# A two-layer decoder trunk on one core: the gate table's one-hot products in fp32r, built four tokens at a time between u tiles

## The reference

```python
D_MODEL, SEQ, DEPTH = 1024, 256, 2
PEER_HEADS, N_KEYS, PEER_TOPK = 8, 128, 16          # 128 x 128 = 16384 experts

def peer_ffn(h, w_query, sub_keys1, sub_keys2, expert_u, expert_v):
    ...
        q = (xb @ w_query).reshape(PEER_BLOCK, PEER_HEADS, 2, PEER_HALF)
        s1 = jnp.einsum('thd,kd->thk', q[:, :, 0], sub_keys1)
        s2 = jnp.einsum('thd,kd->thk', q[:, :, 1], sub_keys2)
        v1, i1 = lax.top_k(s1, PEER_TOPK)
        v2, i2 = lax.top_k(s2, PEER_TOPK)
        cand = (v1[..., :, None] + v2[..., None, :]).reshape(PEER_BLOCK, PEER_HEADS, PEER_TOPK * PEER_TOPK)
        top, ci = lax.top_k(cand, PEER_TOPK)
        idx = (key of half 1) * N_KEYS + (key of half 2)
        gate = jax.nn.softmax(top, axis=-1)
        act = jax.nn.gelu(jnp.einsum('td,tkd->tk', xb, expert_u[idx]))
        return jnp.einsum('tk,tkd->td', gate * act, expert_v[idx])
```

## Time and profile before

| | us |
|---|---|
| median of 3 runs | 2143.91 (2143.36 to 2144.42) |
| the profiled execution, its own time | 2144.6 |
| its span, first to last instruction | 2142.8 |
| TensorE busy | 2086.6, 97% |
| VectorE busy | 1520.0, 71% |
| ScalarE busy | 976.5, 46% |
| GpSimd busy | 778.6, 36% |
| granted TensorE clock, mean | 0.993 |

### The profile page before, as it was taken

One profiled execution on the slowest core, in us unless ns is written; L12 is line 12 of the kernel. 1 busy time (PEld: TensorE's weight loads), 2 busy tenths in 40 slices (PEclk: granted clock), 3 DMA queues, 4 the chain that ended last, 5 costly groups with the idle time before them and its releaser, 6 DMA issues.

```text
span 2142.8 us, 45777 instructions
## 1 busy us (share of the span) xinstructions
PE 2086.6 (97%) x14382; PEld 1943.4 (91%) x14382; DVE 1520.0 (71%) x3212; ACT 976.5 (46%) x1363; POOL 778.6 (36%) x323
## 2 busy tenths in 40 slices
PE   7999999999999999999989999999999999999997
PEld 6999899999998888899889999999999988888996
DVE  3753159789878888777648431797989788886776
ACT  4644454554543333344355444545554433333443
POOL 5698669500000000244367986793000000003442
PEclk9999999999999999999999999999999999999999
DMA  7355457655557777655453554576555687776553
GB/s 234 123 184 183 157 169 227 217 163 161 162 193 245 239 241 242 205 189 185 166 170 127 187 187 149 179 230 203 162 163 160 210 243 241 241 242 194 183 189 120
DMA packets 154706, 410.71 MB, mean 192 GB/s; under 512 B 16987, under 2 KB 67340, under 8 KB 154588
## 3 DMA queue, kind: packets, MB, share of 16 engines
q1 hardware_dynamic: 154220, 407.75, 59.9%
q0 software_dynamic: 368, 1.57, 0.2%
HBM read 382.00 MB, written 27.26 MB: 191 GB/s over the span
## 4 chain that ended last, share of the span: by engine, by line
PE 95%; ACT 1%; DVE 1%; issue 1%; DMA 0%; DVEq 0%; ACTq 0%
PE bank L1048 55%; PE bank L1245 32%; PE bank L1297 5%; PE bank L1223 1%; PE bank L1070 1%; PE bank L1146 0%; PE bank L1103 0%; PE bank L1207 0%; DVE area L748 0%; DVE hT L755 0%; DVE act L976 0%; PE bank L1144 0%; DVE coef L980 0%; DMA x<-in_x 0%; ACT area L485 0%
## 5 line engine op out<-in xcount | busy, mean ns | idle before, releaser
L444 POOL TENSOR_TENSOR halves<-ring,halves 128x1024 fp32r<-128x1024 f32 x308 | 772.4, 2520 | 1327.3 <-ACT halves L509 1325.5
L1048 PE MATMUL bank<-hT,halves 128*128 128x256 f32 x8688 | 1120.6, 285 | 10.8 <-DVE hT L755 9.0
L509 ACT ACTIVATE halves<-ring 128x1024 fp32r<-128x1024 f32 x668 | 707.3, 1060 | 888.0 <-PE bank L1048 468.7
L1048 PEld LDWEIGHTS bank<-hT,halves 128*128 128x128 f32 x8688 | 1068.3, 191 | 18.8 <-issue 9.8
L1245 PE MATMUL bank<-halves,coef 128*128 128x512 f32 x3072 | 711.7, 391 | 3.8 <-DVE coef L982 3.8
L1245 PEld LDWEIGHTS bank<-halves,coef 128*128 128x128 f32 x3072 | 573.3, 188 | 122.6 <-DVE coef L982 5.9
L943 DVE TENSOR_TENSOR halves<-ring,halves 128x1024 fp32r<-128x1024 f32 x360 | 438.9, 1220 | 61.0 <-ACT x L649 25.7
L976 DVE TENSOR_TENSOR act<-act,area 128x256 f32<-128x256 f32 x256 | 223.8, 874 | 99.6 <-ACT act L619 93.9
L956 DVE TENSOR_SCALAR onehot<-ids,x 128x128 f32<-128x128 f32 x512 | 173.7, 339 | 1.9 <-issue 1.9
L1297 PE MATMUL bank<-onehot,x 128*128 128x128 f32 x1024 | 156.0, 274 | 0.0
L955 DVE TENSOR_SCALAR x<-ids,x 128x128 f32<-128x128 f32 x512 | 143.1, 279 | 16.9 <-PE bank L1297 15.9
(11 more groups left out here) (137 smaller groups left out, 951.9 us busy)
## 6 DMA issues: line engine op xcount, KB each, us to landing
ring<-in_stream SPq DMA_DIRECT2D x672, 512.0 KB, 3.5
held_blocks<-act SPq DMA_DIRECT2D x188, 128.0 KB, 1.9
act<-held_blocks SPq DMA_DIRECT2D x188, 128.0 KB, 3.1
area<-rel_scratch SPq DMA_DIRECT2D x2, 1024.0 KB, 6.4
rel_scratch<-act POOLq DMA_DIRECT2D x1, 1532.0 KB, 14.5
area<-in_consts SPq DMA_DIRECT2D x2, 576.0 KB, 3.8
x<-in_x SPq DMA_DIRECT2D x1, 1024.0 KB, 5.0
out_y<-x SPq DMA_DIRECT2D x2, 512.0 KB, 2.7
```

The costliest lines, as they stand in the source:

```text
L444: pool.tensor_tensor(halves[:, s, 1, :], ring[:, s, :], halves[:, s, 0, :].bitcast(F32), ALU.subtract)\
L509: a.activation(halves[:, s, 0, :], ring[:, s, :], ACT.Copy).then_inc(hi_done, 1)
L1048: i = pe.matmul(o, stationary[a], moving[b], start=begin and n == 0, stop=end and n == len(TERMS) - 1)
```

## The change

Five things change together.

1. **The products.** `onehot2` gets a high and a low side: each token's moving operand is 256 columns wide, the gate's fp32r high part in 128 and the low part in the other 128, and the matmul runs in fp32r. The two sides of the result stand beside each other in the bank and are added on the way to `gates_t`: ScalarE copies the high side (`side`), VectorE adds the low side (`add_side`), for two tokens at a time.
2. **The one-hots.** They are made for four tokens at a time (a set, 64 for each layer) by VectorE with `tensor_tensor` on broadcast operands: mask (L992), low side (L996), `onehot1` (L997), weights on the mask's first two tokens (L999). ScalarE puts the weights on the other two (`weighted`). Keys and weights lie in PSUM banks 0 and 1.
3. **The stage.** It holds 64 u tiles in place of 48, one for each set, and GpSimd makes their lows. The main stage has 16 blocks in place of 32. The products' results go to four banks in place of two.
4. **x.** It goes to DRAM behind the mixing (issued on ScalarE's queue), comes back in the main stage, and is added at the end; the identity matmuls go.
5. **Layers.** They are written out in place of the loop.

```diff
-HELD = 48
+HELD = 64
...
+                a.dma_start(x_home, x[:, :, :]).then_inc(x_saved, 16)
...
-                        a.wait_ge(outer_done, l * NQ + j * BODY + (STEPS + 2 * (g4 + 1)))
-                        a.activation(gates_t[:, :, bass.ds(j * (2 * BODY) + 4 * g4, 4)],
-                                     bank_g[g4 % 2][:, :].rearrange("p (t e) -> p e t", t=4), ACT.Copy)\
-                            .then_inc(table_ready, 1)
...
+                def weighted(n):
+                    a.wait_ge(low_placed, l * SETS + n + 1)
+                    for u in range(2, FOUR):
+                        rows = onehot2[:, n % 2, u, 0, :]
+                        i = a.activation(rows, rows.bitcast(F32), ACT.Copy, scale=weight[:, n, u - 2:u - 1])
+                    i.then_inc(onehots_ready, 1)
...
+                def side(q):
+                    a.wait_ge(outer_done, l * NQ + q + 1)
+                    a.activation(gates_t[:, :, 2 * q:2 * q + 2],
+                                 bank_g[q % 4][:, :].rearrange("p (t h e) -> p h e t", t=2, h=2)[:, 0], ACT.Copy)\
+                        .then_inc(side_copied, 1)
...
+                weighted(0)
+                for n in range(SETS):
+                    if n >= 1:
+                        side(2 * n - 2)
+                        side(2 * n - 1)
+                    if n + 1 < SETS:
+                        weighted(n + 1)
+                    hold(n)
...
-                            v.tensor_scalar(onehot1[:, s, u, :], iota, key1, None, ALU.is_equal)
-                            i = v.tensor_scalar(onehot2[:, s, u, :], iota, key2, weight, ALU.is_equal, ALU.mult)
...
+                def add_side(q):
+                    v.wait_ge(side_copied, l * NQ + q + 1)
+                    g2 = gates_t[:, :, 2 * q:2 * q + 2]
+                    v.tensor_tensor(g2, g2, bank_g[q % 4][:, :].rearrange("p (t h e) -> p h e t", t=2, h=2)[:, 1], ALU.add)\
+                        .then_inc(table_ready, 1)
+                def onehots(n, between=None):
+                    if n >= 2:
+                        v.wait_ge(outer_done, l * NQ + 2 * (n - 1))
...
+                    v.tensor_tensor(hi, keys2, numbers, ALU.is_equal).then_inc(mask_ready, 1)
+                    if between is not None:
+                        add_side(between)
+                    v.wait_ge(mask_ready, l * SETS + n + 1)
+                    v.tensor_tensor(lo, hi.bitcast(F32), low_weights, ALU.mult).then_inc(low_ready, 1)
+                    v.tensor_tensor(onehot1[:, n % 2], keys1, numbers, ALU.is_equal)
+                    v.wait_ge(low_ready, l * SETS + n + 1)
+                    v.tensor_tensor(hi[:, 0:2], hi[:, 0:2].bitcast(F32),
+                                    weightT[:, n * FOUR:n * FOUR + 2].unsqueeze(2).to_broadcast([P, 2, NK]), ALU.mult)\
+                        .then_inc(low_placed, 1)
+                onehots(0)
+                onehots(1)
+                for n in range(1, SETS):
+                    if n + 1 < SETS:
+                        onehots(n + 1, 2 * n - 2)
...
+                    add_side(2 * n - 1)
...
+                for n in range(SETS):
+                    held(n)
+                    pe.wait_ge(onehots_ready, l * SETS + n + 1)
+                    for q in (2 * n, 2 * n + 1):
+                        if q >= 4:
+                            pe.wait_ge(table_ready, l * NQ + q - 3)
```

More of the change, by code:

```diff
@@ L341, in _ @@
                 sp.sem_inc(held_stored[k], 16)
-            with sp.Fori(0, DEPTH) as l:
+            for l in range(DEPTH):
                 sp.wait_ge(lo_pool, l * LOP + 1)
@@ L450, in low @@
                 subtract(s)
-            with pool.Fori(0, DEPTH) as l:
+            for l in range(DEPTH):
                 pool.wait_ge(params_ready, l + 1)
@@ L498, in roots @@
                 i.then_inc(root_ready, 1)
-            a.sem_inc(table_ready, 2)
             a.wait_ge(chain, 1)
-            with a.Fori(0, DEPTH) as l:
+            for l in range(DEPTH):
                 g = [0]
@@ L646, in _ @@
                     if s == SEL_AT:
[L647 to L650, removed]
+                        a.wait_ge(sel_turned, l + 1)
+                        a.wait_ge(x_saved, l * 16 + 16)
+                        a.activation(weight_hi, weightT, ACT.Copy).then_inc(weights_hi, 1)
@@ L674, in _ @@
+                side(NQ - 2)
+                side(NQ - 1)
                 for i in range(TAIL):
-                    hold(HELD, i)
+                    hold(HELD + i)
                 with a.Fori(0, EARLY // RING) as r:
@@ L716, in _ @@
             v.tensor_copy(relv, bank[0][:, 0:NDIST]).then_inc(rel_vector, 1)
-            with v.Fori(0, DEPTH) as l:
+            for l in range(DEPTH):
                 links = [1]
@@ L940, in low @@
+                onehots(0)
[3 more added lines that the diff above has]
+                        onehots(n + 1, 2 * n - 2)
+                    else:
+                        add_side(2 * n - 2)
+                    add_side(2 * n - 1)
+                add_side(NQ - 2)
+                add_side(NQ - 1)
                 def low(n, s):
@@ L1022, in _ @@
             pe.wait_ge(rel_vector, 1)
-            with pe.Fori(0, DEPTH) as l:
+            for l in range(DEPTH):
                 g = [0]
@@ L1204, in _ @@
                 pe.wait_ge(taken_v, l * NGV + taken_before(first("h2T"))[0])
-                for t in range(TT):
-                    for hf in range(2):
-                        pe.matmul(acc[2 * t + hf][:, :], ident, x[:, t, hf * HALF_N:(hf + 1) * HALF_N], start=True,
-                                  stop=True)
                 pe.wait_ge(diag_ready, l * 2 + 2)
@@ L1295, in _ @@
+                for n in range(SETS):
[4 more added lines that the diff above has]
+                            pe.wait_ge(table_ready, l * NQ + q - 3)
                         for u in range(2):
-                            o = (2 * q + u) % 4 * NK
-                            i = pe.matmul(bank_g[g4 % 2][:, o:o + NK], onehot1[:, s, u, :], onehot2[:, s, u, :],
-                                          start=True, stop=True)
+                            row = 2 * (q % 2) + u
+                            i = pe.matmul(bank_g[q % 4][:, u * S:(u + 1) * S], onehot1[:, n % 2, row, :],
+                                          onehot2[:, n % 2, row].rearrange("p h k -> p (h k)"), start=True, stop=True)
@@ L1299, in _ @@
                         i.then_inc(outer_done, 1)
-                        for c in range(CHUNKS * q, CHUNKS * (q + 1)):
-                            held(j * PER, c // KD, [c % KD])
                 for i in range(TAIL):
-                    held(HELD, i, range(KD))
-                with pe.Fori(0, EARLY // RING) as r:
+                    held(HELD + i)
+                for s in range(RING):
+                    v_product(s, s, s % 2, opens=s == 0)
+                with pe.Fori(1, EARLY // RING) as r:
```

147 lines of the change are left out of this document (73 added, 74 removed).

## The result

| | us |
|---|---|
| median before, 4 runs | 2144.06 (2143.36 to 2144.42) |
| median after, 4 runs | 2207.52 (2202.33 to 2208.82) |
| ratio, 95% interval | 1.029 (1.0277 to 1.0303) |
| the profiled execution of the kernel after, its own time | 2208.1, span 2206.1 |

The page of the kernel after, parts 1 and 4: busy time by engine, and the chain that ended last.

A forecast was written before the change was run, and what follows sets the result against it. TensorE bound the kernel (busy 97%, 95% of the chain); the change would make a ScalarE-VectorE circle the table stage's pace. 2144.6 - 54 (products) + 108 (waits) + 3 (clock) = 2201 us, range 2160 to 2250.

The forecast's parts named there:

- The products, 54.3 us of gain: Table stage, one-hot products: a pair falls from 0.45 to 0.238 us on TensorE, 256 pairs, 54.3 us less work.
- The work of the others below that: Table stage, one set: VectorE 2.85, ScalarE 2.36, GpSimd 2.4 us of work, all below TensorE's 3.33.
- The circle, 4.25 us: Table stage: ScalarE and VectorE wait for each other, one set each 4.25 us (4.0 to 4.6); chance 0.80.
- A lead of 5 us, a loss of 108: Table stage: TensorE waits 0.92 us for each of 64 sets, less a 5 us lead; 54 us a layer, 108.
- 3 us for the clock at the transposes: Transposes, identity matmuls gone: TensorE idles some 4 us and the clock falls; 1.5 us a layer, 3 in all.
- x through DRAM, written-out layers, 0: Saving and reloading x lies beside other work, bound 0 to 5 us for each layer; written-out layers nothing.
- Vector operations unstretched: Table stage: VectorE's operations with one PSUM operand aren't lengthened by GpSimd's lows; the rival, 2300 to 2430 us, chance 0.05.
- The clock in the stage: Table stage: clock stays 1.00; a rival had it fall at TensorE's stops, 2500 us if throughout, chance 0.03.
- The signs of being wrong: Table stage: no TensorE gaps, 512-column VectorE operations much over 0.69 us, or copies costing more than a 256-column GELU.
- Where TensorE's gap would show: Table stage: TensorE idle 0.9 us in each set ahead of the one-hot products, released by ScalarE's weighting.
- The rival that ended faster: Table stage: copies needn't wait behind high and GELU, circle 3.03 us, TensorE stays the bound; 2094 us, chance 0.09.
- The clock rival: Table stage: TensorE's short stops drop the clock to the 1.2 GHz level; 2500 us throughout, 2300 for a third; chance 0.03.

The follow-up runs named there:

- the second experiment: Against the changed kernel, ScalarE does a tile's high and GELU ahead of the weightings instead of behind them: 2097.45 us.
- the first experiment: Against the changed kernel, VectorE's first adding of a low side is moved from behind the mask to behind the weights: 2092.74 us.
- the dense version: Against the changed kernel, high-side copies and low-side addings work on 256 floats side by side instead of pairs 1 KB apart: 2194.35 us.
- the three versions that break the circle: Against the changed kernel: first adding behind the weights, 2092.74 us; high and GELU ahead of the weightings, 2097.45; VectorE weighting all four tokens, 2097.57.

## Why the prediction was right, step by step

- **TensorE's work was the bound.** Right: with the circle cut, it is again.
- **The products, 54.3 us of gain.** Mis-sized by 3 us. The new pair took 0.24 us, as forecast. But a u matmul takes 0.120 us (2.88/24), not 0.119, so nine of them leave 0.44 of the old step of 1.52 us for the old pair, and 256 x 0.20 = 51 us. The stage says the same: with the circle cut (the second experiment) its pieces take 232.3 us, and 232.3 - 45.9 is 25.5 less than 211.9, in each of two layers. The whole time of the first experiment lies 2145.61 - 2092.74 = 52.9 us below the kernel before (on the same chip), with everything else that changed in it.
- **3.33 us for a set on TensorE.** 3.36 us.
- **The work of the others below that.** Right, and no bound, as the prediction went on to say.
- **The circle, 4.25 us.** 4.30 us, with the same members in the same order. The adding of a side was mis-sized: 0.42 from start to start (504.14 to 504.56) against 0.34, by the order of its accesses; the dense version has 0.34. Small terms the other way (0.59 for the two weightings against 0.62, 1.19 for two operations of 512 columns against 1.22) make up for part of it. High (0.95), low side and `onehot1` (0.59 and 0.60) and the GELU's step (0.27) were the rows' values.
- **A lead of 5 us, a loss of 108.** TensorE's stage was 288.0 us in each layer; with the high first (the second experiment) the same pieces of the chain, 416.04 to 648.34, were 232.3. The loss is 55.7 in each layer, 111 in all, and 64 x 0.94 - 55.7 leaves a lead of 4.5 us. In the timeline TensorE first waits at 435.28, behind the fifth group of products, where the prediction's walk put it. The relay runs from 420.89 to 688.53, 267.6 us against a forecast of some 267. (The 48 tiles of the stage before are a quarter fewer than 64, not a third.)
- **3 us for the clock at the transposes.** In the kernel after, the 32 transposes took 6.78 us in one layer; in the other, 16 of them 3.37, where it was 1.80 before. Between the same two pieces of the chain around them (97.66 to 412.25, before 100.09 to 412.64) a layer is 2.0 us longer, and in the second layer 1.2 (1195.70 to 1509.48, before 1161.20 to 1473.75). Right.
- **x through DRAM, written-out layers, 0.** Right for x. From the first v product to the last product of the main stage, 398.9 us in the first layer (700.28 to 1099.14). That is 128 v tiles at 2.72 and 16 u tiles at 2.87, 394 us, and the gap where the main stage begins, which the kernel before had too. No row waits for x. Elsewhere the profiled execution was 5 us shorter than that of the kernel before: 2.4 ahead of the long piece of the first layer (97.66, before 100.09), and 2.7 behind the first v product of the second (408.7 us to the end of the span, before 457.2, of which 45.9 have moved). No run says which change or which clock they come from.
- **Vector operations unstretched.** Right: 686 to 692 ns for 512 columns all through the stage.
- **The clock in the stage.** It stayed at 1.00 with 0.94 us of stops in each 4.30, so the swing that the Trainium skill ("TensorE: Matmul & The Clock Gate", section on psum-queue depth-cycling) describes did not show in the changed kernel.
- **The signs of being wrong.** One of them showed: the copies cost more than a GELU of 256 columns (439 ns on average against 363). It hardly touched the circle. The first copy lets VectorE start 0.41 us after its own start (503.73 to 504.14), against 0.40 forecast; the second is the long one, 0.49 us (499.70 in the timeline), and lies beside the path.
- **Where TensorE's gap would show.** Wrong in the place: I had it ahead of the one-hot products, released by the weightings. It stands ahead of the u tile (503.97), released by the GELU two tiles back; ahead of the products (506.96) only 0.1 us is left. Both are members of the circle, so the size was untouched.

Between 2201 and 2207.5 lie 6.5 us, and more than one term was off. The stage's loss was 111 in place of 108 and its gain 51 in place of 54, 6 us together. The token mixing of the second layer took 4.8 us more (1105.44 to 1195.70, before 1075.73 to 1161.20), which the forecast did not have, and the 5 us less at other places nearly cancel that: this part of the agreement is luck. Most of the 4.8 us is, in the profiled execution, a clock that fell once more. The attention's logit matmuls of the second layer took, in the chain of the kernel after:

```profile
41.34 4.07 PE bank L1157 x30
...
1134.51 7.53 PE bank L1157 x30
```

and 4.07 in both layers before. (The granted clock was 0.59 and 0.50 from 1134 to 1142, and 1.00 at the same matmuls before.) Over the other profiled kernels the same 30 matmuls took 4.07 us in some layers and 5.7 to 7.4 in others, without an edit that reaches them. It moves a time by 1.6 to 3.5 us, from one execution to the next.

The rival that ended faster was the right one to name: 2094 us was given as the time of a stage in which the queues don't wait for each other, and the three versions that break the circle stand at 2093, 2097 and 2098.

## What to carry to other kernels

Work sums of every engine below the bound say nothing about a pipeline in which two in-order queues wait for each other. Write down, for each engine, the order of its rows and what each waits for, follow the waits until they close, and add up what lies on the circle, from start to start; the number of iterations that it spans divides it. A circle is cut by moving one instruction behind the one that the other engine waits for, at no cost in work, here for 115 us.

A wait costs by what stands behind it in the queue: the wait for the copy, near the head of VectorE's set, held up three operations that did not need it. And an added instruction is priced by its place, free in a wait and paid in full on the circle.

## What the runs showed of the hardware that I had not expected

- With one operation held by GpSimd, a set took 5.64 us (499.68 to 505.32 in the chain). In most sets TensorE's rows are idle for 1.2 us before the products and 0.57 before the u tile; from start to start that is 2.3 us beside 3.36 of work at the upper level. There the granted clock did fall, with no longer stop in the stage, and some u tiles (at 440.21, 457.08, 473.97) took 4.60 us where the others took 3.10:

```profile
430.00:600.00 170.00, 128.81 (x853) 119.52 (x852) 130.36 (x181) 77.21 (x180) 72.86 (x31) 0.90 0.37 118
```

  At 4.30 us a set it stayed at 1.00. The clock rival was thus nearer than its chance of 0.03 said. The Trainium skill ("TensorE: Matmul & The Clock Gate", section on psum-queue depth-cycling) describes such a swing at short, frequent stops between groups of matmuls; this run agrees (0.90), the changed kernel doesn't show it. It cost nothing visible here, since TensorE was not the bound.
- A ScalarE copy of one column behind another operation advances the queue by 0.09 us, though its record is 0.19 us long.
- With pairs of floats 1 KB apart in the table, and the bank read in that order, a ScalarE copy of 256 columns was 0.44 us long in place of 0.37 and a VectorE adding 0.48 in place of 0.42. Where the other engine was not doing so at the same time, they were 0.40 and 0.44.
